# A mixture-of-experts stage: low halves written in place, twelve places for high halves, and the token sorting moved

## What is computed

```python
def moe_swiglu(h, router, wg, wu, wd):       # 256 tokens, D=1024, 8 experts, hidden 3584, top 2
    logits = (t @ router).astype(jnp.float32)
    top_v, top_i = lax.top_k(logits, TOP_K)
    gates = jax.nn.softmax(top_v, axis=-1)
    gate_full = jnp.sum(jax.nn.one_hot(top_i, N_EXPERTS) * gates[..., None], axis=1)
    for e in range(N_EXPERTS):
        out = out + gate_full[:, e:e + 1] * swiglu(t, wg[e], wu[e], wd[e])   # (silu(t@wg) * (t@wu)) @ wd
```

## Time and profile before

| | |
|---|---|
| three runs | 3103.74 us median (3100.64 to 3104.61) |
| the profiled execution | 3096.48 us, its span 3094.7 us |
| PE, DVE, ACT busy | 2879.8, 2287.9, 1651.6 us |
| the stage changed | from 2003.7 us of the span to its end, about 1091 us |
| mean granted TensorE clock | 0.969 |
| DMA | 739.29 MB, of it 758 loads of `moe_raw` of 512 KB |

### The profile page before, as it was taken

How to read it: one execution, slowest core, us unless ns; L and a number is a source line. 1 busy time by engine, 2 the same in 40 slices (tenths; PEclk the granted TensorE clock), 3 DMA queues, 4 the chain that set the end, 5 groups by cost and what they waited for, 6 DMA issues and landing times. The chain is left out here.

```text
span 3094.7 us, 49251 instructions
## 1 busy us (share of the span) xinstructions
PE 2879.8 (93%) x17960; PEld 2375.9 (77%) x17961; DVE 2287.9 (74%) x3284; ACT 1651.6 (53%) x1865; POOL 72.3 (2%) x75
## 2 busy tenths in 40 slices
PE   7999898999999999989889988879998998999988
PEld 3796546898888999977769976668877877888776
DVE  5675754889788666666655567668889889888988
ACT  4354303335534344346344354357778778777886
POOL 0000000000000000000000000000000100000010
PEclk9999899999999999999889999879999999999999
DMA  8570232455687666633145331289999999999997
GB/s 310 204 253 30 106 146 91 144 164 186 257 257 238 201 214 210 213 130 127 57 150 183 122 129 38 107 345 373 364 374 419 397 371 419 394 373 379 390 408 284
DMA packets 228491, 739.29 MB, mean 239 GB/s; under 512 B 23831, under 2 KB 60104, under 8 KB 225480
## 3 DMA queue, kind: packets, MB, share of 16 engines
q1 hardware_dynamic: 222648, 704.49, 62.0%
q0 software_dynamic: 5360, 31.98, 3.1%
q10 hardware_dynamic: 288, 0.26, 0.0%
HBM read 707.28 MB, written 29.36 MB: 238 GB/s over the span
## 5 line engine op out<-in xcount | busy, mean ns | idle before, releaser
L3942 DVE TENSOR_TENSOR moe_lo<-moe_raw,moe_hi 128x2048 fp32r<-128x2048 f32 (+1 forms) x397 | 860.0, 2191 | 125.3 <-ACT moe_hi L3745 123.5
L3745 ACT ACTIVATE moe_hi<-moe_raw 128x2048 fp32r<-128x2048 f32 (+1 forms) x397 | 724.0, 1838 | 245.5 <-PE moe_pB L3611 105.2
L3611 PE MATMUL moe_pB<-moe_hi,moe_hEh 128*128 128x512 f32 x560 | 223.9, 400 | 7.0 <-DVE moe_hEl L4121 5.7
L3611 PE MATMUL moe_pB<-moe_lo,moe_hEh 128*128 128x512 f32 x560 | 220.1, 393 | 0.0
L3611 PE MATMUL moe_pB<-moe_hi,moe_hEl 128*128 128x512 f32 x560 | 219.9, 393 | 0.0
L1971 PE MATMUL exp_pO<-exp_vh,exp_ah 128*128 128x512 f32 x512 | 200.1, 391 | 1.8 <-DVE exp_al L2056 1.8
L1971 PE MATMUL exp_pO<-exp_vl,exp_ah 128*128 128x512 f32 x512 | 200.0, 391 | 0.0
L3623 PE MATMUL moe_pB<-moe_hi,moe_hEh 128*128 128x512 f32 x448 | 182.7, 408 | 18.4 <-DVE moe_lo L3942 17.8
L1971 PE MATMUL exp_pO<-exp_vh,exp_al 128*128 128x512 f32 x512 | 199.2, 389 | 0.0
L1996 ACT ACTIVATE exp_vh<-value_ring 128x1024 fp32r<-128x1024 f32 x128 | 134.8, 1056 | 103.4 <-PE exp_pO L1971 81.5
L2045 DVE TENSOR_TENSOR exp_vl<-value_ring,exp_vh 128x1024 fp32r<-128x1024 f32 x128 | 156.4, 1222 | 30.6 <-ACT exp_vh L1996 28.6
(11 more groups left out here) (861 smaller groups left out, 7268.0 us busy)
## 6 DMA issues: line engine op xcount, KB each, us to landing
moe_raw<-in_moe_w SPq DMA_DIRECT2D x758, 512.0 KB, 7.7
value_ring<-in_peer_v SPq DMA_DIRECT2D x128, 512.0 KB, 4.4
key_ring<-in_peer_u SPq DMA_DIRECT2D x64, 512.0 KB, 3.6
exp_us<-in_peer_u SPq DMA_DIRECT2D x64, 512.0 KB, 5.1
inp_w<-in_w_mod SPq DMA_DIRECT2D x48, 512.0 KB, 7.5
inp_w<-in_w_tiles SPq DMA_DIRECT2D x40, 512.0 KB, 6.2
gates<-route_big POOLq DMA_DIRECT2D x8, 2048.0 KB, 7.2
exp_gs<-gates SPq DMA_DIRECT2D x32, 512.0 KB, 5.7
```

The costliest lines, as they stand in the source:

```text
L3611: i = pe.matmul(pB[:, kind], l[:, kd], m[:, n % HALVES, ns], start=kd == 0 and x == 0, stop=kd == KD - 1 and x == 2)
L3745: act.activation(hi[:, n % HALVES:n % HALVES + count_], raw[:, n % RING:n % RING + count_], ACT.Copy).then_inc(hi_ready, count_)
L3942: dve.tensor_tensor(lo[:, n % HALVES:n % HALVES + count_], raw[:, n % RING:n % RING + count_], hi[:, n % HALVES:n % HALVES + count_], ALU. ...
```

## The change

Three edits, all in `stage_moe`:

1. The low half of a block is written over the raw block itself: `low` is a tensor at the same place as `raw` (21 places), and `lo` is gone. A place of `raw` is free for the next load when PE has used the block, no longer when its low half is made.
2. The space of `lo` goes to `hi`, which has 12 places in place of 6, so that `high` waits for the block 12 back. The counters start at zero; in the first pass loads of the first 21 blocks and spans within the first 12 wait for no counter at all.
3. The sorting steps move. `tables` runs at the stage's begin, ahead of the wait for the token counts; spans 1 and 2 of the first pass (`EARLY` = 3) are converted ahead of the first tokens' copies, with `ranks` ahead of them and `sorted_passes` behind them; `gates` runs behind span 5, without its part for the extra passes; `extras` behind 9, `extra_slots` behind 15, and the rest of the gates (`extra_gates`) behind 19. Three scratch areas move from `sgn` and `prodn` to `hrow`.

```diff
-    RING, HALVES, PRE = 21, 6, 2
+    RING, HIGH, PRE, EARLY = 21, 12, 2, 3
...
-        both = n % RING < RING - 1 and n % HALVES < HALVES - 1
+        both = n % RING < RING - 1 and n % HIGH < HIGH - 1
...
-        hi, lo = sb("hi", [P, HALVES, D], F32R), sb("lo", [P, HALVES, D], F32R)
+        low = nc.alloc_sbuf_tensor_at("moe_low", [P, RING, D], F32R, offset=nc.sbuf_base - RING * D * 4)
+        hi = sb("hi", [P, HIGH, D], F32R)
...
-                    sp.wait_ge(lo_ready, t.at * PASS + n + 1)
+                    if not first_turn(t) or n >= RING:
+                        sp.wait_ge(used, t.at * PASS + (n + 1 + HIGH - RING))
...
-                sp.wait_ge(lo_ready, AHEAD_LO)
...
-                    pe.wait_ge(lo_ready, AHEAD_LO + t.at * PASS + n + 1)
+                    pe.wait_ge(lo_ready, t.at * PASS + (n + 1))
...
-                            for x, (l, m) in enumerate(((hEh, hi), (hEh, lo), (hEl, hi))):
-                                i = pe.matmul(pB[:, kind], l[:, kd], m[:, n % HALVES, ns], start=kd == 0 and x == 0, stop=kd == KD - 1 and x == 2)
+                            for x, (l, m) in enumerate(((hEh, high_of(n)), (hEh, low[:, n % RING]), (hEl, high_of(n)))):
+                                i = pe.matmul(pB[:, kind], l[:, kd], m[:, ns], start=kd == 0 and x == 0, stop=kd == KD - 1 and x == 2)
...
-                    act.wait_ge(used, t.at * PASS + n + count_)
-                    act.activation(hi[:, n % HALVES:n % HALVES + count_], raw[:, n % RING:n % RING + count_], ACT.Copy).then_inc(hi_ready, count_)
+                    if not first_turn(t) or n + count_ > HIGH:
+                        act.wait_ge(used, t.at * PASS + (n + count_))
+                    act.activation(hi[:, n % HIGH:n % HIGH + count_], raw[:, n % RING:n % RING + count_], ACT.Copy).then_inc(hi_ready, count_)
...
                 act.activation(e[:], df[:], ACT.Exp).then_inc(e_ready, 1)
+                for span in SPANS[1:EARLY]:
+                    high(fixed[0], span)
...
-                low(fixed[0], SPANS[0])
...
+                tables()
+                dve.wait_ge(rank_psum, 1)
...
+                def lower(t, span):
+                    n, count_ = span
+                    dve.wait_ge(hi_ready, t.at * PASS + n + count_)
+                    dve.tensor_tensor(low[:, n % RING:n % RING + count_], raw[:, n % RING:n % RING + count_], hi[:, n % HIGH:n % HIGH + count_], ALU.subtract).then_inc(lo_ready, count_)
+
+                lower(fixed[0], SPANS[0])
+                ranks()
+                for span in SPANS[1:EARLY]:
+                    lower(fixed[0], span)
+                sorted_passes()
+
+                PREPARE = {5: gates, 9: extras, 15: extra_slots, 19: extra_gates}
```

More of the change, by code:

```diff
@@ L3425, in after, with first_turn @@
         return Turn(t.at + 1, False, NARROWS if isinstance(t.at, int) else t.number + 1)
+    def first_turn(t):
+        return isinstance(t.at, int) and t.at == 0
     with Stage(nc, "moe") as st:
@@ L3621, in narrow_product @@
                             ns, kd = slice(b * BANK, (b + 1) * BANK), 2 * u + b
-                            for x, m in enumerate((hi, lo)):
-                                i = pe.matmul(pB[:, kind], hEh[:, kd], m[:, n % HALVES, ns], start=kd == 0 and x == 0, stop=kd == KD - 1 and x == 1)
+                            for x, m in enumerate((high_of(n), low[:, n % RING])):
+                                i = pe.matmul(pB[:, kind], hEh[:, kd], m[:, ns], start=kd == 0 and x == 0, stop=kd == KD - 1 and x == 1)
                         i.then_inc(used, 1)
@@ L3664, in narrow_down @@
                             hs = slice(h * BANK, (h + 1) * BANK)
-                            for x, m in enumerate((hi, lo)):
-                                i = pe.matmul(pY[:, h], both[:, u], m[:, n % HALVES, hs], start=g == 0 and u == 0 and x == 0,
+                            for x, m in enumerate((high_of(n), low[:, n % RING])):
+                                i = pe.matmul(pY[:, h], both[:, u], m[:, hs], start=g == 0 and u == 0 and x == 0,
                                               stop=g == GROUPS - 1 and u == UNITS - 1 and x == 1)
@@ L3797, in wide @@
                     for s, span in enumerate(SPANS[1:], 1):
-                        high(t, span)
+                        if s >= EARLY or not first_turn(t):
+                            high(t, span)
                         if s == behind_block(UNITS):
@@ L4020, in gates, with extra_gates @@
                         pick(meta[:, a, 0:NE, 1], gated[:, a])
+                    dve.nop().then_inc(meta_ready, 1)
+                def extra_gates():
+                    over_row = over[:].rearrange("p e j -> p (e j)")
                     for a in range(TT):
@@ L4023, in gates @@
                         pick_extra(meta[:, a, NE:PASSES, 1], over_row)
-                    dve.nop().then_inc(meta_ready, 1)
-                PREPARE = {4: tables, 6: ranks, 8: sorted_passes, 10: extras, 12: extra_slots, 14: gates}
+                tables()
+                dve.wait_ge(rank_psum, 1)
+                c.tick(dve.tensor_copy(count[:], pX[:, 1, 2 * NE:3 * NE]))
+                c.link(dve.tensor_tensor(place[:], pX[:, 1, 0:2 * NE].rearrange("p (a e) -> p a e", a=TT), chosen[:], ALU.mult))
+                c.link(dve.tensor_scalar(place[:], place[:], 1.0, None, ALU.subtract))
+                for a in range(TT):
+                    dve.tensor_scalar(Pz[:, a], io[:], place[:, a, 0:1], None, ALU.is_equal)
+                for a in range(TT):
+                    i = dve.tensor_scalar(Pg[:, a], io[:], place[:, a, 0:1], None, ALU.is_equal)
+                i.then_inc(pg_ready, 1)
+                def lower(t, span):
[8 more added lines that the diff above has]
+                PREPARE = {5: gates, 9: extras, 15: extra_slots, 19: extra_gates}
                 def gathered(t, between):
@@ L4082, in wide @@
                     for s, span in enumerate(SPANS[1:], 1):
-                        low(t, span)
-                        if isinstance(t.at, int) and t.at == 0 and s in PREPARE:
+                        if s >= EARLY or not first_turn(t):
+                            lower(t, span)
+                        if first_turn(t) and s in PREPARE:
                             PREPARE[s]()
@@ L4114, in others @@
                     def others():
-                        low(after(t), SPANS[0])
+                        lower(after(t), SPANS[0])
                     gathered(after(t), others)
```

27 lines of the change are left out of this document (8 added, 19 removed).

## The result

The changed kernel takes 3065.57 us, the median of 4 runs (3060.36 to 3068.66), against 3102.65 us for the kernel before on the same chip (4 runs, 3100.64 to 3104.61). The ratio is 0.9879, 95% interval 0.9861 to 0.9897: 1.2% faster. The forecast was 3057 us, 46.7 less. The profiled execution took 3060.36 us (span 3058.6), 36.1 less than the one of before.

The account below looks back on a forecast made before the run. Wide passes were taken as PE-bound, narrow ones as held by a circle of waits among PE, ACT and DVE. Gains 27.4 + 2.0 + 4.0 + 13.3 = 46.7 us off 3103.7 gave 3057 us, range 3046 to 3082.

Parts of the forecast that it names:

- Narrow passes: Twelve places end most of DVE's waits for ACT: 7.0 us for each of three, 6.4 for the ninth, 27.4 together.
- The second rival: Narrow passes: ACT, held at silu and bank copies, is late again; 14 us less gain, 3071 us; chance 0.15.
- Loads: Ring lends 6.8 us per narrow pass, 13.6 over passes eight and nine; only 1 us lost in the ninth.
- loads become the bound in narrow passes: Rival: the ring lends less, narrow passes stay at 107.7 us, gaining 1 or 2, not 27.4; 3083 us; chance 0.17.
- the slower case: Ring places held too long: decides from landings of 21.6 us; at 22 a narrow pass takes 114.4, total 3110; chance 0.04.
- Wide passes: PE-bound, only the end moves: 0.5 us each in four passes behind the first, 2.0 us (0 to 4).
- The start: From the stage's begin to PE's first product: PE starts at 2024.75, 4.0 us gained, 5.7 at most, 1 at least.
- The first pass: The 6.84 us wait for `meta_ready` and half clock behind it go, sorting stalls cost 5.5; 13.3 us less.

Follow-up runs that it names:

- places6: The changed kernel with 6 places for high halves in place of 12, all else kept; 3094.93 us, ratio 0.9984.
- separate: The changed kernel with seventh pass narrow, eighth wide, and the first extra (ninth) pass taken out ahead of the loop; 3058.47 us, ratio 0.9860.
- rows_late: The changed kernel with the 1 MB copy of `x_tok` to `rows` issued behind block 5's load, not block 1's; 3059.17 us, ratio 0.9866.
- sort_back: The changed kernel with the sorting steps put back behind spans 4, 6, 8, 10, 12 and 14; 3063.40 us, ratio 0.9880.
- all: The changed kernel with separate's edits, rows_late's late copy, and extra-pass sorting behind spans 13, 18 and 22; loop still turned three times; 3057.66 us, ratio 0.9855.
- ring14: The changed kernel with a ring of 14 places in place of 21; 3091.35 us, one run.

## Why the forecast was right where it was, and where it was not

**Narrow passes.** Right in mechanism and size. 7.0 us for each was forecast, 7.6, 6.1 and 9.2 were measured, and 7.6 in all three but for the stretches at half clock; DVE's idle time fell to the 1.6 us in place of the 1.9 that I had left (1.2 and 0.7). places6 shows that it was the places and nothing else. The second rival, in which the wait moves to the order of the program, is out: ACT waits for PE in front of its copies, 9.2 us in the fifth pass, but DVE has work meanwhile. Writing the low halves over their source costs DVE nothing: a span of two takes 2.28 or 2.29 us, as in the earlier trace rows.

**Loads.** This is the step that failed. "5.8 + 13.6 = 19.4, a little over, at the very end, where the last 21 blocks need no successor. Hence the 1 us." It cost 11: 113.2 us measured, 102.0 with a wide pass ahead. I had borrowed from the ring 6.8 us for a narrow pass. The eighth pass moved 405 GB/s x 100.2 us = 40.6 MB of its 45.2, so 4.6 MB or 11 us at 420 were lent: the first five slices of 2.55 us move some 312 GB/s, not 420, and that is 3.3 us that I took as moved. Landings in the eighth were 14.2 in the median and 17.1 at most, with 18 allowed: the ninth began with little left to borrow, and no load in it landed in under 14.3 us. From there on the loads pace it, at the 419 GB/s or so that its slices show but for two at 320, and the last 21 blocks save nothing, since they are the ones that come late. The last load lands 105.1 us behind the begin of the pass, in separate 95.6: that is 9.4 of the 11.2 us, and behind it PE ran 3.4 us at half clock, which separate did not. I treated the end of the kernel as a relief; before, the last load landed at 3070.4 and PE's products ended at 3085.8, so there the relief was real, but the loads were not the bound. Now the two are 3041.2 and 3049.3. The rival "loads become the bound in narrow passes" had the right mechanism for one pass of four; landings reached 19.0 us, not the 21.6 from which the slower case would have begun. The Trainium skill's figure of 358 GB/s for a core ("DMA: Bandwidth & Descriptors", section "Where 436 GB/s comes from"), which the prediction set aside, is set aside by the rows of after too: 414 GB/s through a whole wide pass. Another page of it, "HBM Reference" (section "Specifications (TRN2)"), gives about 425 GB/s for a core that streams alone; with that the trace agrees.

**Wide passes.** 0.5 us each forecast, 0.5 to 0.8 measured. Right.

**The start.** 4.0 us forecast, 2.1 measured. I had the third span's blocks landed and copied at "about 2019" and kept 1 us as the lower bound if they were late. Already the second span's were: ACT started it at 2017.74, behind 3.48 us of waiting for its load, and DVE's two low halves ran from 2019.78 to 2024.49 where I had them from 2016.1 to 2021.3; 1.1 us of that is the later begin of the stage. The 1 MB copy stands in SP's queue ahead of them. rows_late shows it: 20.4 us, 4.6 less than before, near the 4.0.

**The first pass.** 13.3 forecast, 13.5 measured, but the size was met partly by luck, since the attribution was only half right. I put all of it to the sorting. sort_back, with the sorting in its old places, still wins 8.1 us in this pass and 12.7 with the start, because DVE reaches `gates` sooner, by the places, the early spans or both; what the sorting adds is 2.9 us for start and pass together. The details came as forecast: the stalls near block 20 are 1.28 and 0.49 us (1.8 and 0.8 forecast), the 6.84 is gone, the clock is low at the start only.

**Sum.** 46.7 forecast, 36.1 in the profiled executions: 10.1 of the 10.6 us of difference are the ninth pass, 1.9 the start, 1.1 the stage's begin, 0.3 the tail, and 2.8 came out better elsewhere.

**What stays open.** Why a narrow pass behind a wide one starts with five slices at 312 GB/s was not tried. In 2836 to 2849, POOL's row transfers took 20.3% of the time of the 16 DMA engines for 0.52 of the 4.08 MB moved, and SP waited 12 times for PE to use a block, 6.5 us in all; which of the two holds the rate down is not shown. What the twelve places win in the first pass without the early spans is open, and so is why the same wait of 2.61 us is followed by half clock in some narrow passes and not in others.

## What to carry to other kernels

A ring that lends its lead to a pass that wants more than the loads give must have it paid back before the next such pass: count the bytes that the pass really moved, not its top rate, and look at the landing of its last blocks; where two hungry passes follow each other, put the patient one between them (11 us here, for an order of two lists). When two parts of a change hide the same wait, one of them taken back shows little; it takes all four kernels, with everything else the same, and here the fourth was missing. And a bulk copy that nobody waits for does not belong ahead of the loads that the start waits for.

## What the runs showed of the hardware

A loop that is turned three times over a body that never ran cost PE 4.71 and 5.20 us of standing (all, separate); in the changed kernel, where the first turn runs the body, the same place has a wait of 1.3 us, for DVE, and one test over the loop brings that back. But the changed kernel's loop is not free either: DVE stands 2.58 us there for nothing that the profile shows, hidden while PE still multiplies. In ring14, with the same loop, DVE stood 2.40 us, PE waited 3.47 us for it, and the tail was 14.0 us. The Trainium skill ("Runtime: NRT & Kernel Launch", section "Instruction fetch mechanics") says that a taken branch to instructions that are not at hand must fetch them by a DMA before going on. That fits, and by it the test that skips the loop once in place of three times would pay one such fetch; that the 4.71 us are such fetches was not measured.

With a wait of PE of 3.64 us ahead of the first product the granted clock fell to the lower level (3.13 to 3.59 us in four other runs did the same), with one of about 1 us it did not. Behind 2.61 us, near the end of the narrow passes, it fell in some and stayed in others, 1.6 us apart. Behind the 4.71 us the four matmuls of the gather took 3.77 us in place of 1.98. So a long wait at these places is paid for twice, and what shortens it wins more than its length.
